# GpSimd's operations of the second layer in four pieces each, and two query rounds moved into the indexer

## The reference, cut to what matters

```python
q, c, qi, ki, wi = split(h @ w_in)
q = rope(q) * dh ** -0.5                      # 16 heads of 64
c = rms_norm(c, kv_norm); k = rope(c @ w_uk); v = c @ w_uv
qi = rope(qi) * IDX_DIM ** -0.5; ki = rope(ki) # 8 index heads
rel = relu(qi . ki)                            # per index head
score = sum over heads of wi * rel             # causal, else -1e30
_, sel = top_k(score, 256)                     # keys of each query
o = softmax(q . k[sel]) @ v[sel]
```

## Time and profile before

| what | value |
|---|---|
| three runs, median (lowest to highest) | 3380.06 us (3375.84 to 3380.52) |
| the profiled execution's own time | 3380.0 us |
| its span, first to last instruction | 3378.2 us |
| busy PE, DVE, ACT, POOL | 2992.9 (89%), 2085.6 (62%), 1512.3 (45%), 279.4 us (8%) |
| mean granted TensorE clock | 0.937 |
| chain that ended last | PE 77%, DVE 9%, ACT 4%, issue 3%, DMA 3%, POOL 3% |

### The profile page before, as it was taken

One profiled execution on the slowest core, in us unless ns is written; L12 is line 12 of the kernel. 1 busy time (PEld: TensorE's weight loads), 2 busy tenths in 40 slices (PEclk: granted clock), 3 DMA queues, 4 the chain that ended last, 5 costly groups with the idle time before them and its releaser, 6 DMA issues.

```text
span 3378.2 us, 37432 instructions
## 1 busy us (share of the span) xinstructions
PE 2992.9 (89%) x13312; PEld 2299.4 (68%) x13312; DVE 2085.6 (62%) x3708; ACT 1512.3 (45%) x2609; POOL 279.4 (8%) x221
## 2 busy tenths in 40 slices
PE   7797999999879999999968664389997999999997
PEld 5685666666667888878856553256666788887885
DVE  6544445555266766677675699664326676667656
ACT  4342554455444544444433544344434454444443
POOL 2352000000000000000003035300000000000000
PEclk9787999999989999999989787689998999999999
DMA  5143211121322333333323012332132233333332
GB/s 165 44 105 97 50 47 39 42 52 36 110 75 88 95 93 100 95 92 96 98 69 96 0 54 84 94 70 54 39 104 75 88 94 94 100 95 93 99 109 73
DMA packets 360178, 270.45 MB, mean 80 GB/s; under 512 B 63942, under 2 KB 313864, under 8 KB 359480
## 3 DMA queue, kind: packets, MB, share of 16 engines
q1 hardware_dynamic: 358839, 265.96, 27.4%
q10 hardware_dynamic: 1152, 2.10, 0.2%
HBM read 233.46 MB, written 29.82 MB: 78 GB/s over the span
## 4 chain that ended last, share of the span: by engine, by line
PE 77%; DVE 9%; ACT 4%; issue 3%; DMA 3%; POOL 3%; SPq 1%; POOLq 0%; ACTq 0%; DVEq 0%
PE PS L485 18%; PE PS L487 18%; PE PS L486 18%; PE PS L890 10%; PE PS L813 3%; PE PS L868 3%; PE PS L866 3%; PE PS L872 2%; SPq L1912 1%; DVE m_Z L2285 1%; DVE RT_b L590 1%; DMA WL<-ql_save 1%; POOL m_QS L1929 1%; PE PS L639 1%; PE PS L884 0%
## 5 line engine op out<-in xcount | busy, mean ns | idle before, releaser
L485 PE MATMUL PS<-HH,WH 128*128 128x512 f32 (+1 forms) x2160 | 859.1, 398 | 133.9 <-POOL WL L458 90.3
L486 PE MATMUL PS<-HL,WH 128*128 128x512 f32 (+1 forms) x2160 | 850.7, 394 | 0.0
L487 PE MATMUL PS<-HH,WL 128*128 128x512 f32 (+1 forms) x2160 | 849.6, 393 | 0.0
L485 PEld LDWEIGHTS PS<-HH,WH 128*128 128x128 f32 x2160 | 415.9, 193 | 228.2 <-issue 96.9
L486 PEld LDWEIGHTS PS<-HL,WH 128*128 128x128 f32 x2160 | 415.5, 192 | 87.1 <-issue 2.5
L487 PEld LDWEIGHTS PS<-HH,WL 128*128 128x128 f32 x2160 | 414.4, 192 | 86.6
L474 DVE TENSOR_TENSOR WL<-WR,WH 128x1024 fp32r<-128x1024 f32 x290 | 354.2, 1221 | 109.4 <-ACT WH L467 97.8
L467 ACT ACTIVATE WH<-WR 128x1024 fp32r<-128x1024 f32 x290 | 308.1, 1062 | 124.4 <-PE PS L487 89.9
L910 ACT ACTIVATE n_PX<-PS 128x512 f32<-128x512 f32 (+3 forms) x400 | 186.7, 468 | 256.7 <-PE PS L872 205.3
L1002 DVE CUSTOM_DVE_ANT_0 n_JUNK<-PS,n_MZ 128x512 bf16<-128x512 f32 (+2 forms) x320 | 148.6, 488 | 134.1 <-PE PS L813 132.6
L454 POOL TENSOR_TENSOR TOUCH<-WR 128x1 f32<-128x1 f32 x45 | 12.0, 267 | 2030.4 <-PE PS L487 1031.3
(11 more groups left out here) (375 smaller groups left out, 5373.3 us busy)
## 6 DMA issues: line engine op xcount, KB each, us to landing
WR<-in_ffn_w_up SPq DMA_DIRECT2D x176, 512.0 KB, 3.8
WR<-in_ffn_w_down SPq DMA_DIRECT2D x88, 512.0 KB, 3.6
WH<-qh_save SPq DMA_DIRECT2D x64, 256.0 KB
n_RB<-r_save SPq DMA_DIRECT2D x96, 128.0 KB, 3.0
WR<-in_nsa_w_out SPq DMA_DIRECT2D x16, 512.0 KB, 4.1
WL<-ql_save SPq DMA_DIRECT2D x32, 256.0 KB
WR<-in_dsa_w_in SPq DMA_DIRECT2D x16, 512.0 KB, 4.4
WR<-in_dsa_w_out SPq DMA_DIRECT2D x16, 512.0 KB, 4.2
```

The source lines that it names most:

```text
L485: nc.tensor.matmul(dst, wh, xh, start=start, stop=False)
L486: nc.tensor.matmul(dst, wh, xl, start=False, stop=False)
L487: return nc.tensor.matmul(dst, wl, xh, start=False, stop=stop)
```

## The change

1. GpSimd's operations on query rounds run as four operations of 128 elements each in place of one of 512 (`QUARTERS`), and the weight splits for rounds 4 to 15 as four of 256 in place of one of 1024, for the high and for the low part (`split_in_parts`). The semaphore is incremented by the last piece.
2. Rounds 0 and 1 (`EARLY = 2`) are projected by TensorE between the scores of the third and of the fourth head pair. ScalarE copies them behind ReLU 2 and ReLU 5 of the fourth pair. The high part of round 0 is written behind the last ReLU, before ScalarE's increment of `a_ready`.
3. In the search bit 0 copies round 2 in place of round 0, and so on: the last copy is in bit 26, the last high part in bit 29, and none is left behind the search. The low part of round 1 waits for the last scores, since its buffer holds index queries until then.

```diff
--- before.py
+++ after.py
@@ -457,6 +457,22 @@
             pool.wait_ge(w_hi, at(info["n"], it) + 1)
             nc.gpsimd.tensor_tensor(WL[:, s, :], WR[:, r, :], WH[:, s, :].bitcast(F32),
                                     ALU.subtract).then_inc(w_split, 1)
+
+        def split_in_parts(pool, info):
+
+            r, s = info["raw"], info["split"]
+            pool.wait_ge(w_raw[r], info["landed"])
+            pool.wait_ge(*info["free"])
+            nc.gpsimd.tensor_tensor(TOUCH[:, :], WR[:, r, 0:1], WR[:, r, 0:1], ALU.mult)
+            for c in range(0, T, 2 * P):
+                last = nc.gpsimd.tensor_scalar(WH[:, s, c:c + 2 * P], WR[:, r, c:c + 2 * P], 1.0, 0.0,
+                                               ALU.mult, ALU.add)
+            last.then_inc(w_hi, 1)
+            pool.wait_ge(w_hi, info["n"] + 1)
+            for c in range(0, T, 2 * P):
+                last = nc.gpsimd.tensor_tensor(WL[:, s, c:c + 2 * P], WR[:, r, c:c + 2 * P],
+                                               WH[:, s, c:c + 2 * P].bitcast(F32), ALU.subtract)
+            last.then_inc(w_split, 1)
 
         def high_split_act(act, info):
 
@@ -1868,6 +1884,9 @@
         def query_turned(k):
             return M["VT"][:, 1, :] if k % 2 else M["ROT"][:, 0:HALF]
 
+        EARLY = 2
+        QUARTERS = [slice(P * x, P * x + P) for x in range(4)]
+
         def query_part(part, k):
             flat = M["QS"][:, :, :, :].rearrange("p s h n -> p (s h n)")
             o = HALF * (2 * part + k % 2)
@@ -1924,21 +1943,33 @@
 
             def query_low_part(k):
                 pool.wait_ge(a_qhi, a.q0 + k + 1)
+                if k == 1:
+                    pool.wait_ge(S["sc"], 48)
                 if k >= 2:
                     pool.wait_ge(a_saved[k % 2], a.saved0 + 32 * (k // 2))
-                nc.gpsimd.tensor_tensor(query_part(1, k), query_value(k),
-                                        query_part(0, k).bitcast(F32), ALU.subtract).then_inc(a_qlo, 1)
+                for c in QUARTERS:
+                    last = nc.gpsimd.tensor_tensor(query_part(1, k)[:, c], query_value(k)[:, c],
+                                                   query_part(0, k)[:, c].bitcast(F32), ALU.subtract)
+                last.then_inc(a_qlo, 1)
 
             for k in range(ROUNDS):
-                value, turned, tok = query_value(k), query_turned(k), tokens(k % 2)
+                value, turned, h0 = query_value(k), query_turned(k), HALF * (k % 2)
                 pool.wait_ge(S[f"turn{k % 2}"], 64 * (k // 2 + 1))
-                nc.gpsimd.tensor_tensor(value, value, M["COS"][:, tok], ALU.mult).then_inc(a_t1, 1)
-                nc.gpsimd.tensor_tensor(turned, turned, M["SIN"][:, tok], ALU.mult).then_inc(a_t2, 1)
+                for c in QUARTERS:
+                    last = nc.gpsimd.tensor_tensor(value[:, c], value[:, c],
+                                                   M["COS"][:, h0 + c.start:h0 + c.stop], ALU.mult)
+                last.then_inc(a_t1, 1)
+                for c in QUARTERS:
+                    last = nc.gpsimd.tensor_tensor(turned[:, c], turned[:, c],
+                                                   M["SIN"][:, h0 + c.start:h0 + c.stop], ALU.mult)
+                last.then_inc(a_t2, 1)
                 pool.wait_ge(a_t1, a.q0 + k + 1)
                 pool.wait_ge(a_t2, a.q0 + k + 1)
-                nc.gpsimd.tensor_tensor(value, value, turned, ALU.add).then_inc(a_qf, 1)
+                for c in QUARTERS:
+                    last = nc.gpsimd.tensor_tensor(value[:, c], value[:, c], turned[:, c], ALU.add)
+                last.then_inc(a_qf, 1)
                 if k % 2 and k // 2 + 2 < PAIRS:
-                    split(pool, L1["q"][k // 2 + 2])
+                    split_in_parts(pool, L1["q"][k // 2 + 2])
                 if k >= 1:
                     query_low_part(k - 1)
             query_low_part(ROUNDS - 1)
@@ -2027,10 +2058,12 @@
                 transposes(2 + hf)
             queries(3)
             scores(2, 0, 12)
+            pe.wait_ge(S["cn"], 3)
+            for k in range(EARLY):
+                project_queries_pe(pe, A1, k, 4 + k % 4)
             scores(3, 0, 12)
-            for k in range(ROUNDS):
-                if k == 0:
-                    pe.wait_ge(S["cn"], 3)
+            for k in range(EARLY, ROUNDS):
+                if k == EARLY:
                     pe.wait_ge(S["t1"], 8)
                 if k >= 4:
                     pe.wait_ge(a_rot, A1.q0 + k - 3)
@@ -2147,10 +2180,22 @@
                     values(0)
                 if n == 5:
                     values(1)
+            def query_copy(k):
+                act.wait_ge(proj, a.q0 + k + 1)
+                if k >= 2:
+                    act.wait_ge(a_qlo, a.q0 + k - 1)
+                nc.scalar.activation(query_value(k), bank(4 + k % 4), ACT.Copy,
+                                     scale=0.125).then_inc(a_rot, 1)
+
             for n in range(12):
                 relu(3, n)
-            act.wait_ge(S["acc"], 48)
-            act.sem_inc(a_ready, 1)
+                if n == 2:
+                    act.wait_ge(S["rl"], 8)
+                    act.wait_ge(S["sc"], 36)
+                    query_copy(0)
+                if n == 5:
+                    act.wait_ge(S["vtr"], 4)
+                    query_copy(1)
 
             def query_high_part(k):
                 act.wait_ge(a_qf, a.q0 + k + 1)
@@ -2158,6 +2203,9 @@
                     act.wait_ge(a_saved[k % 2], a.saved0 + 32 * (k // 2))
                 nc.scalar.activation(query_part(0, k), query_value(k), ACT.Copy).then_inc(a_qhi, 1)
 
+            query_high_part(0)
+            act.wait_ge(S["acc"], 48)
+            act.sem_inc(a_ready, 1)
             for bit in range(31):
                 act.wait_ge(S["cand"], bit + 1)
                 for i in ACT_TILES:
@@ -2165,22 +2213,16 @@
                                                 ACT.Sign, bias=M["CAND"][:, i - 2:i - 1], scale=-1.0,
                                                 accum_out=M["CNT"][:, i - 2:i - 1])
                 last.then_inc(S["sgn"], 1)
-                k = bit // 2
-                if bit % 2 == 0:
-                    act.wait_ge(proj, a.q0 + k + 1)
-                    if k >= 2:
-                        act.wait_ge(a_qlo, a.q0 + k - 1)
-                    nc.scalar.activation(query_value(k), bank(4 + k % 4), ACT.Copy,
-                                         scale=0.125).then_inc(a_rot, 1)
-                elif k >= 1:
+                k = EARLY + bit // 2
+                if bit % 2 == 0 and k < ROUNDS:
+                    query_copy(k)
+                elif bit % 2 and k <= ROUNDS:
                     query_high_part(k - 1)
                 if 16 <= bit < 28 and bit % 2 == 0:
                     i = 2 + (bit - 16) // 2
                     act.wait_ge(S["signed"], 1)
                     nc.scalar.activation(tile_of("Z", i), tile_of("Z", i), ACT.Copy,
                                          scale=M["SG"][:, i - 2:i - 1]).then_inc(S["signed"], 1)
-            query_high_part(14)
-            query_high_part(15)
             for i in (2, 3):
                 mask_act(act, i)
```

## The result

The changed kernel takes 3390.69 us (median of nine runs, 3387.12 to 3392.54), the kernel before 3379.66 beside it. The ratio is 1.0032, 95% interval 1.0022 to 1.0043: 11.0 us slower. The forecast was 3392.7.

The account below looks back on a forecast made before the run. The cycle of query rounds, not VectorE, was taken to set the pace between indexer and attention. 15.1 + (174.7 - 178.2) + 1.1 = +12.7 us made the span 3390.9 and the forecast 3392.7 us, range 3374 to 3400.

Parts of the forecast that it names:

- four pieces, start to start: GpSimd's query operations: four 128-element pieces take 1.64 us against 1.22 for one whole operation, at 0.14 us an instruction.
- plain step, step with a split: Distance between ScalarE's round copies in the search: 11.5 us without a weight split, 15.8 with one, from 9.8 and 13.3.
- VectorE's idle time behind the projections: End of the indexer: 48 projection matmuls delay the last head pair's scores, so VectorE starts that block 9.3 us later.
- copies among the ReLUs and pieces beside accumulates: End of the indexer: ScalarE's two copies add 0.5 us, GpSimd's pieces meeting the last six accumulates add 1.8 us.
- backlog of GpSimd before copy 2: Start of the search: copy 2 waits for GpSimd's queued work, starting 15.1 us after copy 0 did; backlog's share 2 us.
- the two steps over the change of halves: Where VectorE goes from upper to lower half of the bits: 33.3 us becomes 31.0, L2397 taking about 7.6 us.
- copy 15 to attention's first matmul: End of the search: TensorE starts 25.2 us after copy 15 instead of 24.1, +1.1 us, the search now being late.
- the sum told in other words: Whole stage: two rounds and a split (23.1 us) leave; pieces add 22.1, the indexer 13, GpSimd's backlog 2.
- rival of free pieces: GpSimd's rounds: issue is hidden, pieces cost nothing, so -12.4 us in place of +12.7, 3367.6 us; chance 0.14.
- rival of half the price: Pieces cost half, or the indexer hides half of the projections: +0.2 or +8 us, 3380 to 3388; chance 0.18.
- the lock's case: Search rounds: VectorE's small two-input operations hold up GpSimd's pieces, +1.4 us a round, 18 over 13 rounds, 3411 us; chance 0.08.
- estimate of 0.06 us for an instruction: GpSimd's fixed price from the skill page's figures; the sum would be -1.6 us instead of +12.7; prediction took 0.14.

Follow-up runs that it names:

- e3: Kernel before with TensorE's projections of rounds 0 and 1 moved ahead of the last head pair's scores, nothing else; 3389.62 us, ratio 1.0027.
- e2: Changed kernel with every GpSimd operation whole again, so only the early rounds remain; 3372.73 us, ratio 0.9977.
- e8: Chunked-projection kernel (pieces in rounds 0 and 1), with pieces also in round 9, its split and the low part of round 8; 3368.14 us, ratio 0.9967.
- e1: Kernel before with GpSimd's operations in four pieces, in its own order, nothing moved; 3401.52 us, ratio 1.0063.
- e5: Changed kernel with query operations in eight pieces of 64 elements, weight splits still in four; 3423.75 us, ratio 1.0132.
- e6: Changed kernel with query operations in two pieces of 256 elements, weight splits still in four; 3379.89 us, ratio 1.0001.
- e7: As e4, with the two projections cut in 16 chunks of three matmuls between score groups; 3370.38 us, ratio 0.9976.
- e4: Changed kernel with pieces only in rounds 0 and 1 and the split behind round 1, whole operations from round 2; 3372.95 us, ratio 0.9979.
- e9: As e8, but pieces only in round 0 and at the change of halves; round 1 and the split behind it whole; 3369.41 us, ratio 0.9968.

## Why the prediction was right

Its steps, each against the trace of the changed kernel:

| step | predicted | measured |
|---|---|---|
| four pieces, start to start | 1.64 us | 1.68 us |
| plain step, step with a split | 11.5, 15.8 us | 11.5, 15.9 us |
| VectorE's idle time behind the projections | 9.3 us | 9.2 us (e3 alone: +9.8 us of time) |
| copies among the ReLUs and pieces beside accumulates | 0.5 + 1.8 us | 0.8 us: 12.8 us of block in place of 11.95 |
| scalings, copy and small operations beside pieces | 1.5 us | 1.9 us: 13.3 from the first count to the search in place of 11.4 |
| backlog of GpSimd before copy 2 | 2.0 us | 2.7 us |
| copy 2 to copy 15 | 174.7 us | 174.3 us |
| of it the two steps over the change of halves | 31.0 us | 29.45 us |
| copy 15 to attention's first matmul | 25.2 us | 26.1 us |
| sum over the stage | +12.7 us | +12.7 us |

That the sum agrees to a tenth is luck of errors that cancel; the medians differ by 11.0. The mechanism, four pieces at 1.68 us in every step, is not luck. Three of the terms were off:

- A piece beside accumulates costs VectorE next to nothing: six of them took 7.49 us, and 2 x (1.02 + 1.15 + 1.28) = 6.9 alone by the groups of this line, so 0.1 each in place of 0.3. It is GpSimd that waits, 4.43 us for four pieces. A whole operation costs VectorE 0.8 us an accumulate (11.63 in e2).
- At the change of halves the operation took 5.65 us in place of 7.6, near the 5.2 to 5.6 that the prediction had for it undisturbed. GpSimd's pieces did meet its second half, and as beside the accumulates it is they that waited (four took 3.73 us in place of 1.69). The wait of 0.3 us a part was the wrong way round in both places. In e8, where pieces meet all of it, it took 6.45.
- Behind copy 15 I missed that ScalarE scales a tile of `m_Z` in bit 26 too (1.14 us, L2224), ahead of the counts that VectorE waits for. It was within bit 26 before as well, but off the path.

Two places of the working do not come out. The prediction's 7.6 us for the masks is not 10.2 less the 1.9 blocked, as it reads; the trace has 7.5 (2174.49 to 2181.95), so the figure held and its working did not. And the sum told in other words leaves out the 2.3 us won at the change of halves and the 1.1 behind copy 15.

The step that decided was the price of a piece. The rival of free pieces would have made the kernel 12 us faster. e1, e5 and e6 rule it out: e1 adds nothing but pieces and costs 21.7 us; e6 with two, the change with four and e5 with eight pieces stand at +0.5, +11 and +44 us. The rival of half the price falls with them, and its other form, projections half hidden, with e3 (+9.8 us). In the changed kernel GpSimd's pieces are not held up much by VectorE's small operations either (four pieces take 1.68 to 1.73 us all through the search, but for the four that meet the change of halves), so the lock's case did not come. The estimate of 0.06 us for an instruction, worked out from the figures in the Trainium skill, GPSIMD Engine Reference, section 3.1, does not hold in this case; the runs decide for 0.14 to 0.15.

That both parts pull in opposite directions is shown by e1 and e2: early rounds -7.1, pieces +18 on top. The forecast's account for the early rounds, 23 us leaving and 13 + 2 coming back in the indexer, is borne out by e2's trace (22.6 and 15.1 us), and e3 says that 9.8 of the loss is TensorE's order. The time of e2 is 7.1 us less and its stage, in one trace, only 4.2, since behind copy 15 it lost 3.4; the rest of the difference stays open.

## What to carry to other kernels

Before cutting operations of an engine to let another one in, find which of the two the stretch waits for: here the cut engine was in the cycle that set the pace for 174 of 240 us, and the one it spared was on the path in three short places only: the end of the indexer, the change of halves and the end of the search. Of these, cutting gained 3.3 us in the traces at the change of halves (e8 against e7); at the end of the indexer GpSimd's backlog took the gain back (e4); the third was not tried by itself. Work moved forward in an in-order queue delays all behind it by nearly its whole length when the consumers are only two buffers deep (9.2 us of idle time for 10.9 us of matmuls); in chunks between the consumers' groups half of that came back here, and the rest stayed because TensorE was then full. And take an instruction's fixed price from distances between starts of operations of several sizes: three rows told the steps of the kernels with two, four and eight pieces to 0.1 us (10.4, 11.5 and 13.8).

## What was not expected of the hardware

- When VectorE and GpSimd hold each other up, short and long operations do not lose alike. Beside back-to-back accumulates of about 1.1 us, four pieces of GpSimd take 4.43 us in place of 1.68 and VectorE loses 0.1 us an operation. Beside whole operations of 1.26 us, VectorE loses 0.8 us an operation and GpSimd's take 1.96 to 2.28. Halves lie between: VectorE loses 0.3 us an operation (8.88 us for six in e6).
- VectorE operations with a single SBUF input collide too, if they are the fast ones: the six scalings took 3.06 us alone, 3.86 to 3.88 beside pieces (changed kernel, e4, e7, e8), 5.30 in e6 and 7.00 beside the whole split and low part (e9), and four 256-element pieces of a split took 4.12 us in place of 1.51 beside the last scaling and the copy to halves. The counting operations, about as long per element as an accumulate (1.01 and 1.02 us for 768), met GpSimd all through the search at their usual 0.61 to 1.01 us.
